# The pre-norm scale of a decoder trunk as a row: by a store and a broadcast load instead of two transposes

## What is computed

```
def rms_norm(x, g, eps=NORM_EPS):
    xf = x.astype(jnp.float32)
    y = xf * lax.rsqrt(jnp.mean(xf * xf, axis=-1, keepdims=True) + eps)
    return (y * g.astype(jnp.float32)).astype(x.dtype)

def swiglu(x, w_gu, w_down):
    g, u = jnp.split(x @ w_gu, 2, axis=-1)
    return (jax.nn.silu(g) * u) @ w_down

    f = swiglu(rms_norm(h, ffn1_pre_g[i]), ffn1_w_gu[i], ffn1_w_down[i])
    h = h + 0.5 * rms_norm(f, ffn1_post_g[i])
    u = rms_norm(h, mix_pre_g[i])
    sb_q, sb_k, sb_v, df_q, df_k, df_v, g_sb, g_df = jnp.split(u @ w_in[i], split_at, axis=-1)
```

## Time and profile before

| | |
|---|---|
| time, median of 3 runs | 1173.87 us |
| span of the profiled execution | 1172.6 us |
| lowest and highest run | 1173.72 and 1174.38 us |
| TensorE matmul busy (PE) | 1164.0 us, 99% |
| TensorE weight load busy (PEld) | 983.8 us, 84% |
| VectorE busy (DVE) | 850.0 us, 72% |
| ScalarE busy (ACT) | 721.0 us, 61% |
| bytes moved by DMA | 215.37 MB, mean 184 GB/s |

### The profile page before, as it was taken

How to read it: one execution, slowest core, us unless ns; L and a number is a source line. 1 busy time by engine, 2 the same in 40 slices (tenths; PEclk the granted TensorE clock), 3 DMA queues, 4 the chain that set the end, 5 groups by cost and what they waited for, 6 DMA issues and landing times.

```text
span 1172.6 us, 17196 instructions
## 1 busy us (share of the span) xinstructions
PE 1164.0 (99%) x6031; PEld 983.8 (84%) x6031; DVE 850.0 (72%) x1290; ACT 721.0 (61%) x1166; POOL 53.0 (5%) x124
## 2 busy tenths in 40 slices
PE   9999999999999999999999999999999999999997
PEld 7888888888888888888888888888888888888886
DVE  6766776977857776676787776678776677677666
ACT  7555556577755755555685655565776566565555
POOL 4000000000000000000100000010000010000002
PEclk9999999999999999999999999999999999999999
DMA  9656564654354555655556565746434446546550
GB/s 296 217 181 212 171 215 164 226 172 152 121 201 146 191 204 185 208 174 211 179 171 198 172 211 179 240 165 198 171 111 179 162 162 215 194 170 209 179 196 37
DMA packets 138655, 215.37 MB, mean 184 GB/s; under 512 B 6958, under 2 KB 97904, under 8 KB 138608
## 3 DMA queue, kind: packets, MB, share of 16 engines
q1 hardware_dynamic: 135808, 208.43, 52.6%
q10 hardware_dynamic: 2576, 6.29, 1.6%
q0 software_dynamic: 224, 0.04, 0.0%
HBM read 213.68 MB, written 1.05 MB: 183 GB/s over the span
## 4 chain that ended last, share of the span: by engine, by line
PE 99%; DMA 0%; DVE 0%; ACT 0%; issue 0%; POOL 0%; POOLq 0%; DVEq 0%; ACTq 0%
PE ps L1673 23%; PE ps L1546 19%; PE ps L1548 18%; PE ps L1547 18%; PE ps L1683 12%; PE ps L1916 3%; PE ps L1593 1%; PE ps L1925 1%; PE ps L1802 1%; PE ps L1817 1%; PE ps L1776 0%; PE ps L1788 0%; DMA raw<-in_w_ple_proj 0%; PE ps L1831 0%; PE ps L1838 0%; PE ps L1803 0%
## 5 line engine op out<-in xcount | busy, mean ns | idle before, releaser
L1106 DVE SCALAR_TENSOR_TENSOR w_lo<-raw,g_layer,w_hi 128x512 fp32r<-128x512 f32 (+1 forms) x504 | 356.3, 767 | 139.2 <-ACT w_hi L644 139.2
L644 ACT ACTIVATE w_hi<-raw,g_layer 128x512 fp32r<-128x512 f32 (+1 forms) x524 | 346.7, 732 | 113.6 <-PE ps L1683 97.0
L1673 PE MATMUL ps<-x_both,w_hi 128*128 128x512 f32 x1152 | 287.7, 392 | 0.0
L1673 PEld LDWEIGHTS ps<-x_both,w_hi 128*128 128x128 f32 x1152 | 209.3, 189 | 39.4 <-issue 0.4
L1546 PE MATMUL ps<-w_hi,x_both 128*128 128x512 f32 x576 | 231.6, 402 | 0.0
L1548 PE MATMUL ps<-w_hi,x_both 128*128 128x512 f32 x576 | 225.0, 391 | 0.0
L1547 PE MATMUL ps<-w_lo,x_both 128*128 128x512 f32 x576 | 224.4, 390 | 0.0
L1103 DVE TENSOR_TENSOR w_lo<-raw,w_hi 128x1024 fp32r<-128x1024 f32 x114 | 134.8, 1221 | 61.3 <-ACT w_hi L641 61.3
L641 ACT ACTIVATE w_hi<-raw 128x1024 fp32r<-128x1024 f32 x114 | 114.7, 1053 | 92.7 <-PE ps L1548 92.5
L1683 PEld LDWEIGHTS ps<-x_both,w_lo 128*128 128x128 f32 x1152 | 152.6, 191 | 8.4
L1683 PE MATMUL ps<-x_both,w_lo 128*128 128x256 f32 x1152 | 156.0, 283 | 0.0
(11 more groups left out here) (230 smaller groups left out, 1041.7 us busy)
## 6 DMA issues: line engine op xcount, KB each, us to landing
raw<-in_ffn_w_gu SPq DMA_DIRECT2D x170, 512.0 KB, 4.6
raw<-in_ffn_w_down SPq DMA_DIRECT2D x88, 512.0 KB, 4.0
raw<-in_w_in SPq DMA_DIRECT2D x80, 512.0 KB, 4.5
raw<-in_w_out SPq DMA_DIRECT2D x16, 512.0 KB, 4.1
raw<-in_w_ple_gate SPq DMA_DIRECT2D x16, 512.0 KB, 4.1
raw<-in_w_branch_sb SPq DMA_DIRECT2D x8, 512.0 KB, 4.1
raw<-in_w_branch_diff SPq DMA_DIRECT2D x8, 512.0 KB, 4.2
raw<-in_ffn_w_gu SPq DMA_DIRECT2D x12, 256.0 KB, 7.8
```

Source lines behind the costliest of these rows:

```text
L644: last = act.activation(w_hi[:, s, part], raw[:, s, part], ACT.Copy, scale=g_layer[:, g:g + 1])
L1106: last = dve.scalar_tensor_tensor(out=w_lo[:, s, part], in0=raw[:, s, part], scalar=g_layer[:, g:g + 1], in1=whi[:, part], op0=ALU.mult, o ...
L1673: mm = pe.matmul(dst, w_hi[:, s, cols], x_both[:, :, 4 * half + k, :], start=half == 0 and k == 0, stop=stop and k == 3, skip_group_check= ...
```

## The change

The row now goes through device memory. `store_r`, issued by ScalarE, writes the 256 numbers of `r_pre` to a row of a small tensor in device memory (`r_rows`), each partition giving two numbers of 4 bytes that land 128 numbers apart. `load_r`, also issued by ScalarE, waits for that store and loads the row back into `r_cols`, the same 1 KB for each of 128 partitions. The VectorE copy, the two transposes, the ScalarE copy and TensorE's waits for `r_kept` go. In an FFN the store is issued as soon as the scale of the second token tile is known, and the load stands where the ScalarE copy stood. In the mixer the store stands ahead of block 0, and the load behind block 2.

```
+        r_rows = nc.dram_tensor("r_rows", (3 * DEPTH, SEQ), F32, kind="Internal").ap()
...
-            def keep_r(i, stage, b=R_BANK):
-                act.wait_ge(r_turned, nth_r(i, stage))
-                act.activation(r_cols[:, 0, :], bank(b)[:, 0:SEQ], ACT.Copy).then_inc(r_kept, 1)
+            def store_r(i, stage):
+                act.dma_start(r_rows[nth_r(i, stage) - 1, :].rearrange("(t p) -> p t", p=P), r_pre[:, :]
+                              , allow_slow_non_contiguous=True).then_inc(r_stored, 16)
+
+            def load_r(i, stage):
+                act.wait_ge(r_stored, 16 * nth_r(i, stage))
+                act.dma_start(r_cols[:, 0, :], r_rows[nth_r(i, stage) - 1, :].partition_broadcast(P)
+                              ).then_inc(r_kept, 16)
...
                 act.wait_ge(pre_scale, 8 * i + 4 * f + 2)
+                store_r(i, 2 * f)
                 silu(i, f, 0, u0 + 1, 1)
                 high(i, u0 + 3, g0 + 4, halves=(1,))
                 high(i, u0 + 4)
-                keep_r(i, 2 * f)
+                load_r(i, 2 * f)
                 high_first_ht(i, f)
...
                     if m == 2:
-                        keep_r(i, 1, QK_PAIR)
+                        load_r(i, 1)
...
                 act.wait_ge(pre_scale, 8 * i + 4)
+                store_r(i, 1)
                 mixer(i)
...
                 product(i, f, 0, 1)
-                spread_r(i, (i, f) == (0, 0))
...
-                dve.wait_ge(r_kept, nth_r(i, 2 * f))
+                dve.wait_ge(r_kept, 16 * nth_r(i, 2 * f))
                 flat_gate(i, f, 1)
...
             def turn_first_ht(i, f):
-                turn_r(i, 2 * f, R_BANK)
...
-                    if first:
-                        pe.wait_ge(r_kept, nth_r(i, 2 * f))
                     down(u0 + 1, c - 1, first=first, c=at)
...
-                if m == 2:
-                    turn_r(i, 1, QK_PAIR)
                 if m == 4:
-                    pe.wait_ge(r_kept, nth_r(i, 1))
                     pe.wait_ge(roped, 4 * i + 2)
```

More of the change, by code:

```diff
@@ L175, in trunk_kernel @@
         glu_g, glu_u = glu[:, 0, :, :], glu[:, 1, :, :]
-        r_spread = mixed_t[:, 0:SEQ].rearrange("p (t n) -> p t n", t=TT)
         r_cols = prob[:, 0:1, 0:SEQ]
+        r_rows = nc.dram_tensor("r_rows", (3 * DEPTH, SEQ), F32, kind="Internal").ap()
         e_ple = gates[:, 1, :, :]
@@ L204, in trunk_kernel @@
         h_done = sem("h_done")
-        r_wide = sem("r_wide")
-        r_turned = sem("r_turned")
+        r_stored = sem("r_stored")
         r_kept = sem("r_kept")
@@ L309, in trunk_kernel @@
         FLAT_BANK = (6, 7, 4, 5)
-        FIRST_HT_BANK, R_BANK = 2, 3
+        FIRST_HT_BANK = 2
         flat_g, flat_u = ([ps[:, b:b + 2, n * SEQ:(n + 1) * SEQ] for n in range(2)] for b in FLAT_BANK[::2])
@@ L1139, in low_ht @@
                                   ).then_inc(ht_split, 1)
-            def spread_r(i, first=False):
-                if first:
-                    dve.wait_ge(const_all, 1)
-                dve.tensor_copy(r_spread, r_pre[:, :].rearrange("p (t o) -> p t o", o=1).to_broadcast([P, TT, P])
-                                ).then_inc(r_wide, 1)
             def flat_gate(i, f, c):
@@ L1329, in add_flat @@
                 dve.wait_ge(flat_added, n)
-                dve.wait_ge(r_kept, nth_r(i, 1))
+                dve.wait_ge(r_kept, 16 * nth_r(i, 1))
                 dve.tensor_tensor(dst, dst, r_cols.to_broadcast([P, 2, SEQ]), ALU.mult).then_inc(sb_ready, 1)
@@ L1336, in mixer @@
                 dve.wait_ge(pre_scale, 8 * i + 4)
-                spread_r(i)
                 dve.wait_ge(query_scale, i + 1)
```

## The result

| | before | after |
|---|---|---|
| median, same chip, 5 runs each | 1174.18 us | 1184.07 us |
| lowest and highest | 1173.72 to 1174.38 | 1181.62 to 1185.39 |
| profiled execution: time, span | span 1172.6 us | 1184.4 us, span 1182.7 us |

The ratio after to before is 1.0084 [1.0072, 1.0096]: the change makes the kernel slower by 0.84%, 9.9 us. The forecast was 1172.6 us with a range up to 1174.8, so it is wrong, and on the wrong side. What happened is rival A (0.07) and rival C (0.08) together, and neither at its price: with a store of 10.4 us, A by the prediction's working would have cost 2 x (10.4 - 9.7) = 1.4 us, and C was put at 1.6.

A forecast was written before the change was run, and what follows sets the result against it. TensorE's queue of matmuls bounds the kernel (99% of the chain); 12 fewer transposes save 1.3 us, the copies nothing, and the new waits stay hidden: 1173.87 less 1.3 is 1172.6 us, range 1171.2 to 1174.8.

The forecast's parts named there:

- rival A: The store blocks ScalarE, with the high parts queued behind it; a 12 us store would give 1177.2 us; chance 0.07.
- rival C: Late row, partly paid: store and load 7.8 us each, 0.8 us lost at first and third FFN, 1174.2 us; chance 0.08.
- The six pairs: TensorE's 12 removed transposes, 0.21 us a pair in four FFNs and 0.22 in two mixers: 1.3 us gained.
- Rival B: The transposes on TensorE were hidden by the weight queue or a later wait: no change, 1173.9 us; chance 0.09.
- rival D: TensorE's transpose pairs cost their modelled 0.38 us each: 2.3 us gained, 1171.6 us; chance 0.08.
- the store's issue of 0.38 us: On ScalarE ahead of the silu, which has 1.0 us to spare before VectorE's product, so the issue fits.
- the store's term: First FFN: the store takes 5.8 us from r at 26.2 and lands at 32.0, 0.2 us after ScalarE would go on.
- The second failed term: First FFN: the load takes 5.0 us, the row lands at 37.0, VectorE is 0.5 us late and this is hidden.
- the prediction's own working: The row's path in the FFNs: row wanted at 36.5, 4.5 us left before TensorE waits; lateness beyond this adds to the span.
- The 34.1 us: First FFN, ScalarE: end of the hidden tile's low part, instead of 33.53; TensorE asks at 37.60, 3.5 us left.
- The decision point of a blocked ScalarE: First and third FFN: a store over 9.7 us, landing after 35.9 us, uses up the hidden tile's slack.
- `w_lo` at 48.46: First FFN: TensorE asks for the next unit's low part at 48.46, which ends at 43.95; 4.5 us are left.

The follow-up runs named there:

- the kernel without store: The changed kernel without its six stores; ScalarE loads the row from an input vector without a wait: 1172.53 us, ratio 0.9988 to before.
- the 256 pieces of 512 bytes: The changed kernel storing 256 pieces of 512 bytes side by side, the load waiting and reading an input vector: 1172.84 us, ratio 0.9989 to before.
- the pairs: The changed kernel storing 128 pieces of 8 bytes, two scales per partition, VectorE reading at step two: 1172.82 us, ratio 0.9989 to before.
- the two-piece store: The changed kernel storing its 1 KB as 2 x 512 bytes from a tile of ones: 1172.73 us, ratio 0.9989 to before.

## Why the prediction was wrong

**The queue and its sum were right.** The six pairs were summed to 1.3 us by starts. The mixer stages came out at -0.25 us each against 0.22 forecast, and the seven kernels without the transposes that have a quick store into device memory, or none, run 1.1 to 1.5 us under before. The span forecast, 1171.3, was met by the kernel without store (1171.3); each run's time lies some 1.7 us above its own span and not 1.3, so that this span would have meant 1173.0. The Trainium skill's rule of the weight loads' share ("Perfetto Trace Analysis", Identifying the Most-Contended Engine), by which a removed transpose could be worth less, did not hold: the share was 84% and the gain was whole. Rival B (hidden transposes) and rival D (2.3 us) fall with that. VectorE's and ScalarE's copies were worth nothing, and the store's issue of 0.38 us fitted ahead of the silu: TensorE starts its wide products 27.80 - 25.02 = 2.78 us after r_pre, as before (28.44 - 25.66).

**The step that failed is the store's term:** "I take 5.8, the row nearest in size of piece", with 7.8 as the upper bound. It measured 10.4, of which 5.7 to 6.6 in the FFNs came after its last packet. The rows of the bound were all loads into the chip or a store of whole rows, none had many small writes to neighbouring bytes, and I let the largest of them stand as an upper end although it resembled the store in nothing. The Trainium skill's figure was no part of the sum and would have been further off ("DMA: Bandwidth & Descriptors", Anatomy of one DMA: some 2 us fixed, given there for DMAs that GpSimd issues): the estimate from it was 4 us for store and load together, where 19 us were measured, and 9.4 + 6.9 us with GpSimd as the issuer. That most of it is the wait for the last write to be confirmed agrees with the dense store, which spends 5.7 to 6.6 us there, and not with the quick ones, with 0.4 to 1.1. The same page's rule of one descriptor per element points at the right place, but the count of pieces is not the cause, as the 256 pieces of 512 bytes show.

**The second failed term is the load:** "A load of exactly this shape took 5.0 us", upper bound 7.8. It measured 8.7, and 3.8 without the store (from an input vector). The row was read where the queues were calm, while here the load is issued when what the store held back begins to move. The DMA engines around the store of the second FFN, issued at 391.79 and landed ahead of 401.39 (columns as above):

```profile
391.80:394.00 2.20, 2.20 (x11) 1.80 (x11) 0.57 (x2) 2.07 (x4) 0.00 (x0) 1.00 0.89 259
394.00:396.00 2.00, 2.00 (x12) 1.69 (x11) 1.91 (x4) 1.92 (x4) 0.00 (x0) 1.00 0.73 230
396.00:398.00 2.00, 2.00 (x13) 1.78 (x13) 2.00 (x3) 1.68 (x2) 0.00 (x0) 1.00 0.00 0
398.00:401.30 3.30, 3.30 (x25) 3.10 (x25) 1.50 (x2) 0.00 (x0) 0.00 (x0) 1.00 0.18 42
...
404.00:407.00 3.00, 3.00 (x15) 2.47 (x14) 2.35 (x4) 1.29 (x3) 0.00 (x0) 1.00 1.06 385
```

Up to 396 us the engines finish the two weight loads issued ahead of the store, as quickly as ever (4.0 and 4.9 us). The 0.00 of the third row is no sign of anything: no weight load is out from 396.0 to 397.4, and before, the share is 0.00 at the same place too. The sign is the fourth row: of the loads that SyncE issues at 397.39 and 397.95 little moves (42 GB/s) until the store has landed, and afterwards the engines are full (1.06). These two land after 8.3 and 9.3 us, the next two, issued at 399.68 and 400.22, after 9.1 and 11.3; before, the same four took 3.9 to 5.1.

The crowd may not be all of it. With the pairs, the load of the second FFN is issued at 392.75, 0.25 us ahead of the next weight load, and takes 5.6 us; behind the two-piece store, at the same place and also from `r_rows`, it takes 2.8. So reading back a row that was written in small pieces may itself be slow. Where the load read an input vector behind a quick store (4.1 to 4.5 us), its source had changed as well, and no run separates the two. What makes the load long stays open.

**With the measured durations the prediction's own working gives the result.** It said that the row's path from r may be 14.8 us (41.0 - 26.2) in the first and third FFN and 2.5 us more in the others. Store and load measured, FFN by FFN, 10.1 + 9.0, 9.6 + 9.2, 10.8 + 9.0 and 10.2 + 8.5 us: late by 4.3, 1.5, 5.0 and 1.4, in sum 12.2. Then 1173.9 - 1.3 + 12.2 = 1184.8 us, and 1184.07 was measured. The stages lost (with 0.21 for each pair added back) 4.93, 1.20, 4.76 and 1.12 us. The fit of the first FFN has some luck in it: 1.6 us of its 4.93 is the granted clock, which the working did not have. It is also luck that the sum fits so well with all of the lateness put at one place: TensorE in fact paid it at three (`ht_lo`, the wide products, `w_lo`).

**Smaller steps were off.** ScalarE was to go on at 31.8 without the copy; without a store it starts L710 at 32.02, as the four transposes in front of it end no earlier. The 34.1 us for the end of the low part counts the 0.4 us of the load's issue twice; by the same rows it is 32.4 + 0.63 + 0.69 = 33.7. Neither changes the forecast. The decision point of a blocked ScalarE was set at a store of 9.7 us, but the load's own issue (0.34, and a gap) stands between the store's landing and the hidden tile. It is 9.3: TensorE started its first `down` late by 2.69 - 1.84 = 0.85 us with a store of 10.1 (34.89 to 37.58, against 1.84 for such eight matmuls with no wait behind them, 49.92 to 51.76). And I had looked for TensorE's first wait at the next unit, `w_lo` at 48.46. It comes earlier, at the wide products that start at 43.04 before, because L1152 frees their banks and stands behind the wait for the row. The slack there is a little larger (L1152 could start at 42.3 instead of 36.72), so `w_lo` was the tighter one by about a microsecond, and TensorE pays it as a remainder, 0.37 us in three places.

**Chances.** A's mechanism was named, with its condition of a store of 11.5 us for a measurable loss; the loss came already at 10.4, because the load on the row's path was late too. Its 0.07 rested on "the slowest group of DMAs in this trace took 7.8 us", an argument from transfers of another kind. An unseen kind of transfer with its completion awaited on a full pipeline deserved a range to well over 10 us.

**Shown and not shown.** Shown: without the store and its wait there is no loss; its slowness goes with dense small pieces and goes away with distance or with larger pieces; it lies between the last packet and the completion; the loss passes through ScalarE's stand and the late row; the mixers hide it. Inferred only: that the writes into one block of memory have to follow one another. The Trainium skill says that a transfer of under 512 bytes makes the DMA engine read, modify and write ("DMA: Bandwidth & Descriptors", Specifications). If such writes to one block are serial, this agrees with the order of the rows of the table, and with the 4-byte pieces 64 bytes apart, which cost nothing extra. It is not a matter of their count alone, since half as many pieces cost a fifth of the excess. No run here shows the reads, or how large the block is beyond this: 64 bytes apart is enough.

## What to carry to other kernels

Price a DMA by its landing pattern too, and not by its bytes: a short vector that crosses partitions should leave in one piece, in a few long ones, or at least spread apart, and a reader with a step can take it in that order, which cost nothing here. A completion wait put into a busy engine's queue costs whatever stands behind it, and a slow store delays transfers that have nothing to do with it. Where the trace has no row of the same kind as a new transfer, the largest other row is no upper bound.

## What was unexpected of the hardware

- 256 writes of 4 bytes side by side in device memory landed after 10.4 us, and the same 64 bytes apart after 5.1 us. In the FFNs the dense store's packets had all started 5.7 to 6.6 us before it landed, those of pieces 64 bytes or more apart, or 512 bytes long, 0.4 to 1.1 us before.
- Such a store holds back other queues: weight loads that SyncE issued in its last 4 us landed after 8.3 to 11.3 us instead of 3.9 to 5.1, with the DMA engines at a share of 0.18 meanwhile. Those issued ahead of it were not slowed (4.0 and 4.9 us). Issued by GpSimd the store is about as slow (9.4 us).
- The granted clock fell to 0.50 after 2.15 us of idle TensorE in the first FFN (with 0.69 us of idle time 8 us before) and stayed at 1.00 in the third, after 2.14 us (with 1.41 us before). I tried nothing on what tells the two apart.
- The issue of the store or the load on ScalarE took 0.33 to 0.44 us in after, but 0.61 to 0.69 us for 4-byte pieces into an on-chip tile.
